# A conditioned decoder layer on one core: cache pages issued three per early gate tile, one operand cut ahead of an evacuation, one activation column behind the exponentials

## The chip, the cores and the metric

One core of a Trainium2 chip runs the whole program. The metric is the device time of that core in microseconds, the median of several runs. TensorE is written PE, VectorE DVE, ScalarE ACT, GpSimd POOL and SyncE SP; ACTq and SPq are the queues on which ACT and SP issue DMAs.

## What is computed

One step of a decoder layer for 256 prompt tokens and 8 sequences of 4 sample tokens, 288 token columns in all, with D_MODEL = 1024 and everything in float32. Cut to what matters here:

```python
h = rms_norm(x, g_norm1) * (1 + scale1) + shift1
q, k, v, qi, ki, wi, u_conv, gates = split(h @ w_in)        # u_conv = [a | g]
z = a * sigmoid(g)                                          # branch B: GLU, then a causal conv of width 31
attn = sparse_attention(q, k, v, qi, ki, wi, cache pages)   # branch A; the samples read 2 cached pages per sequence
x = x + gate1 * ((sigmoid(gA) * (attn @ w_o) + sigmoid(gB) * conv_out) @ w_out)
h2 = rms_norm(x, g_norm2) * (1 + scale2) + shift2
# PEER: 16 picks per head out of 128 x 128 experts
s1, s2 = scores of h2 @ w_q_peer against sub_keys1, sub_keys2
top_s, top_j = top_k(all sums of the best 16 of s1 and of s2, 16)
gate = softmax(top_s)                                       # needs Exp
act = gelu(u_emb[eid] @ h2)                                 # needs Gelu
x = x + gate2 * sum(gate * act * v_emb[eid])
```

The kernel computes the activations of all 16384 experts densely, 128 tiles of 128 experts, and picks afterwards.

## The kernel before

Everything is written by hand, one instruction stream per engine, ordered by semaphores. A weight tile is 128 x 1024 floats (512 KB). SP streams the tiles into a ring of four (`ring`), and the load of a tile waits until the tile four places earlier is done (`tile_done`).

**The head.** `HEAD` is the order of the first products: for k = 0 to 5 the pairs conv_a k, conv_g k, then ki and the four qi tiles, conv_a and conv_g 6 and 7, then v, k and q. After every second tile one tile ("ada", g, s) of the conditioning weights is put in; four of them (s = 0 to 3) make a group g. PE, `linear`, writes tiles other than conv_a alternately into two PSUM banks (`BANK`), and `free` makes PE wait until the tile two places earlier in that order has been evacuated. ACT follows the same list `HEAD`:

- behind a conv_g tile it applies the sigmoid (line 810) and then issues the DMAs of two cache pages, 2m and 2m + 1 for tile m (`load_page`, lines 795 to 797: a register load and four DMAs per page, 32 + 32 + 128 + 128 KB; 16 pages in all);
- behind the last tile of a conditioning group it copies the group (`group_copy`, line 759). PE may not begin the next group before that: `later_ada` waits with `pe.wait_ge(ada_copied, g)`. Group 4 ends behind conv_g 3, and the first tile of group 5 stands behind conv_g 4;
- PE turns the group through a bank (`turn_group`), and ACT copies it out (`turned_copy`, line 765). The turn of group 4 stands behind conv_g 5, ahead of ki; its bank is wanted next by qi 0.

ACT's instructions and the DMAs it issues form one stream in program order. DVE multiplies a and sigmoid(g) (line 1142) and runs the prompt convolution in four pairs of channels (lines 1151, 1155).

**From the PEER queries to the scores.** The 16 tiles peer_q are multiplied in three passes (`linear_cut`: high part by high, high by low, low by high). ACT cuts the high part of a tile into `split` (`cut_tile`, line 781), POOL subtracts it for the low part (line 648), and ACT evacuates each product (`evac`, line 771). Behind the last one PE scores the queries against the sub-keys (line 2072), ACT copies these scores (lines 975, 980), and only then cuts the high part of the first u tile (`cut_high(0, ...)`, line 991). PE needs that high part for `scores(0)` (lines 2095, 2096), and POOL's low part (`cut_low`, line 683) for the last pass (line 2102). PE also waits, ahead of `scores(0)`, for both copies `pscore_copied` and `s_pscore_copied`. `split` has two slots; slot 0 is that of peer_q 14 and of u tile 0, slot 1 that of peer_q 15 and of u tile 1.

**The u tiles.** In each turn of four ACT cuts the next tile's high part and applies gelu to the finished one (line 1020). Behind 16 tiles it applies Exp to the three groups of picks (line 1033), and a loop of three turns follows. The picks' tables are worked out by DVE meanwhile, and PE needs them behind 28 tiles.

Of the kernel before, what the change touches and what calls it, by code (L numbers as in the profile page):

```python
# [21 lines left out]
TP, NSEQ, TD = 256, 8, 4  # L22
# [10 lines left out]
PAGE, NPAGES = 128, 2  # L33
# [78 lines left out]
NRING = len(LOADS)  # L112
# [15 lines left out]
def loaded(pos):  # L128

    return 16 * ((pos - NWIDE) // R + 1)  # L130


def slot_of(c):

    return (NRING + c) % R


def loads_before(c):

    return (NRING + c - NWIDE) // R  # L140
# [27 lines left out]
def tokens(t):  # L168

    return (slice(t * P, t * P + P), P) if t < NQ else (slice(TP, T), TS)  # L170


def build(nc, a):
    f32, f32r, bf16 = mybir.dt.float32, mybir.dt.float32r, mybir.dt.bfloat16
    i32, u32 = mybir.dt.int32, mybir.dt.uint32
    ALU, ACT, AX = mybir.AluOpType, mybir.ActivationFunctionType, mybir.AxisListType

    with ExitStack() as ctx:
        def sb(name, *shape, dt=f32):
            return ctx.enter_context(nc.sbuf_tensor(name, [P] + list(shape), dt))  # L180

        def sem(name):
            return ctx.enter_context(nc.semaphore(name))


        ring = sb("ring", R, D)

        split = sb("split", 2, 2, D, dt=f32r)
# [134 lines left out]
        late = Region(big, NBIG)  # L323
# [10 lines left out]
        tv = late.take(NT, PH, PTOP)  # L334
# [3 lines left out]
        gsum = late.take(NT, PH, 2)  # L338
        eq = late.take(PH * PTOP, PTOP)
        s_expert = late.take(2, TS)  # L340
        assert late.at <= NSUB * TP


# [44 lines left out]
        tile_loaded = [sem(f"tile_loaded{s}") for s in range(R)]  # L388
# [6 lines left out]
        tile_done = sem("tile_done")  # L395
        v_done = sem("v_done")
        u_done = sem("u_done")
        bank_done = sem("bank_done")
        o_done = sem("o_done")
        hi_ready = sem("hi_ready")  # L400
        lo_ready = sem("lo_ready")
        hi_used = sem("hi_used")
# [10 lines left out]
        x_stored = sem("x_stored")  # L413
# [93 lines left out]
        top_exp = sem("top_exp")  # L507
# [109 lines left out]
        def _(pool):  # L617
# [54 lines left out]

            low_tiles(("peer_q",))

            pool.wait_ge(tile_done, NRING)


            def cut_low(c, n, used, value=None):
                pool.wait_ge(hi_ready, c + 1)
                if value is not None:  # L680

                    pool.wait_ge(used, value)
                nc.gpsimd.tensor_tensor(split[:, n % 2, 1], ring[:, slot_of(n), :], split[:, n % 2, 0].bitcast(f32),  # L683
                                        ALU.subtract).then_inc(lo_ready, 1)

            for n in range(R):
                cut_low(n, n, u_done, n - 1 if n >= 2 else None)
            with pool.Fori(1, NSUB // R) as g:
                for n in range(R):
                    cut_low(g * R + n, n, u_done, g * R + (n - 1))  # L690
# [33 lines left out]
        def _(eng):  # L724
# [28 lines left out]
            def group_copy(g):  # L753

                eng.wait_ge(tile_done, POS["ada", g, R - 1] + 1)
                if g >= NFIRST + 2:

                    eng.wait_ge(group_turned, g - NFIRST - 1)
                nc.scalar.activation(m_row2[:, g % 2], adab[:, 0:P], ACT.Copy).then_inc(ada_copied, 1)
# [9 lines left out]
            def evac(key, dst, func=ACT.Copy):  # L769
                eng.wait_ge(tile_done, POS[key] + 1)  # L770
                nc.scalar.activation(dst, lin[BANK[key]][:, 0:T], func).then_inc(act_evac, 1)  # L771

            def cut_tile(key):

                n, at = CUT.index(key), POS[key]
                eng.wait_ge(tile_loaded[at % R], loaded(at))
                if n >= 2:

                    eng.wait_ge(lin_hi_used, n - 1)
                    eng.wait_ge(lin_lo, n - 1)  # L780
                nc.scalar.activation(split[:, n % 2, 0], ring[:, at % R, :], ACT.Copy).then_inc(lin_hi, 1)  # L781
# [17 lines left out]
            for key in HEAD:  # L799
                kind, m = key[:2]  # L800
                if kind == "conv_a":
                    continue
                if kind == "ada":
                    if key[2] == R - 1:
                        group_copy(m)
                elif kind == "turn":
                    turned_copy(m)
                elif kind == "conv_g":
                    eng.wait_ge(tile_done, POS[key] + 1)
                    nc.scalar.activation(sig[:, m], lin[BANK[key]][:, 0:T], ACT.Sigmoid).then_inc(sig_ready, 1)  # L810

                    eng.wait_ge(pages_in, 16)
                    for n in (2 * m, 2 * m + 1):
                        load_page(n)
                elif kind == "ki":
                    evac(key, ki)
                elif kind == "qi":
                    evac(key, qi[:, m])
                elif kind == "v":
                    eng.wait_ge(v_done, m + 1)  # L820
                    rows = tokens(m)[1]
                    nc.scalar.activation(vtok[0:rows, m], lin[BANK[key]][0:rows, 0:VW], ACT.Copy)\
                        .then_inc(act_evac, 1)
                else:
                    n = QK.index(key)
                    if n == len(QK) - 1:
                        cut_tile(("gate_a", 0))
                    evac(key, kT[:, m] if kind == "k" else q[:, m])
                    evac(key, sq_qk[n], ACT.Square)
                    if key == ("q", 3):  # L830

                        eng.wait_ge(z_ready, 2 * KC)
                        nc.scalar.activation(staged_s, zs[:, :, :, TD:TD + LEFT], ACT.Copy).then_inc(conv_staged, 1)
                        nc.scalar.activation(staged_p, zp[:, :, TP:TP + LEFT], ACT.Copy).then_inc(conv_staged, 1)
# [56 lines left out]
            for n in range(NQ * H + 2):  # L891
# [13 lines left out]
                if 1 <= n <= NQ * H:  # L905
                    m = n - 1
# [6 lines left out]
                if n >= 2:  # L913
                    m = n - 2
# [38 lines left out]
            for k in range(KC):  # L953
                eng.wait_ge(h2_ready, k + 2)
                nc.scalar.activation(hi_all[:, k, 0:TP], h2[:, k, 0:TP], ACT.Identity, bias=mod[:, 3, k, 0:1])\
                    .then_inc(rhs_hi, 1)

            eng.wait_ge(stored, 16 * 4)
            for n in range(2 * PH):
                if n + 1 < 2 * PH:  # L960
                    cut_tile(("peer_q", n + 1))
                evac(("peer_q", n), qh[:, n])
                if n == 0:
                    for i in range(2):
                        eng.wait_ge(late_done, i + 1)
                        nc.scalar.activation(m_row2[:, i], pa[1 + i][:, 0:P], ACT.Copy).then_inc(late_copied, 1)
                if n == 2:
                    eng.wait_ge(late_turned, 1)
                    nc.scalar.activation(mod[:, 5], pa[3][:, 0:2 * P].rearrange("p (c g) -> p c g", g=CW_ADA)[:, :, 0:NG],
                                         ACT.Copy).then_inc(late_mod, 1)  # L970
                if n % 4 == 3:
                    for t in range(NQ):
                        m = n // 4 * NQ + t
                        eng.wait_ge(pscore, m + 1)
                        nc.scalar.activation(sc[:, t, n - 3:n + 1], pa[m % 4][:, :].rearrange("p (a b) -> p a b", b=NSUB),
                                             ACT.Copy).then_inc(pscore_copied, 1)
                    if n % 8 == 7:
                        pair = n // 8
                        eng.wait_ge(s_pscore, pair + 1)
                        nc.scalar.activation(sc[:, NQ, 2 * pair:2 * pair + 2],  # L980
                                             (adab, stb)[pair][:, 0:2 * NSUB].rearrange("p (a b) -> p a b", b=NSUB), ACT.Copy)\
                            .then_inc(s_pscore_copied, 1)

            def cut_high(c, n, loaded, first=False):

                eng.wait_ge(tile_loaded[slot_of(n)], loaded)
                if not first:

                    eng.wait_ge(hi_used, c - 1)
                    eng.wait_ge(lo_ready, c - 1)  # L990
                nc.scalar.activation(split[:, n % 2, 0], ring[:, slot_of(n), :], ACT.Copy).then_inc(hi_ready, 1)  # L991

            def gelu(c, n, first=False):

                eng.wait_ge(u_done, c + 1)
                if not first:

                    eng.wait_ge(act_stored[n % 2], 32 * (c // 2))
                nc.scalar.activation(act[:, n % 2], ps[n % 2][:, 0:T], ACT.Gelu_apprx_tanh).then_inc(gelued, 1)

            def first_of(n):
                return 16 * (loads_before(n) + 1)


            eng.wait_ge(x_stored, 16)
            eng.wait_ge(tile_done, NRING)
            cut_high(0, 0, first_of(0), True)
            for c in range(R):
                cut_high(c + 1, (c + 1) % R, first_of((c + 1) % R) + 16 * ((c + 1) // R), c == 0)
                gelu(c, c, c < 2)  # L1010
# [20 lines left out]
            for t in range(NT):  # L1031
                eng.wait_ge(top_max, t + 1)
                nc.scalar.activation(tv[:, t, 0:HEADS[t]], tv[:, t, 0:HEADS[t]], ACT.Exp).then_inc(top_exp, 1)
            with eng.Fori(SOFTMAX // R, TURN // R) as g:
                turn(g, False)

# [1256 lines left out]
```

## Time and profile before

| | us |
|---|---|
| median of 3 runs | 1268.54 (1267.66 to 1269.44) |
| profiled execution, its own time | 1270.7 |
| span of the profiled execution, first to last instruction | 1268.9 |
| busy in it: PE | 1226.8 (97%) |
| DVE | 923.4 (73%) |
| ACT | 570.6 (45%) |
| POOL | 550.5 (43%) |

Times in the rows below are microseconds from the span's start. A row of the timeline has the start, the duration, the engine, the line, the operation with output and input, the count of instructions merged, and in brackets how long the engine had been idle ahead of it and what ended that. ACT_TABLE_LOAD is ACT's change of its function table, with the line of the activation that it is for. "issue" in the brackets means that nothing in the profile was waited for: the engine's own stream had not reached the instruction.

### The profile page before, as it was taken

To read this page: it belongs to the slowest core of one execution; us is meant where nothing else is said; L and a number is where in the kernel's file an instruction comes from. 1 tells how busy PE (TensorE), PEld (TensorE's weight loads), DVE (VectorE), ACT (ScalarE), POOL (GpSimd) and SP (SyncE) were. 2 spreads that over 40 slices of the span, in tenths; PEclk is the share of its full clock that TensorE was granted. 3 is DMA by queue.
4 is the path that set the end of the run, shared out by engine and by line. 5 is a ranking of instruction groups with operands and counts; after the bars stand their busy time and mean duration, and the time that the engine had idled before them with its cause. 6 is when DMAs were issued, how large, how long until landed. Compare 5 with 4: busy or idle time off the path is not lost.

```text
span 1268.9 us, 27584 instructions
## 1 busy us (share of the span) xinstructions
PE 1226.8 (97%) x8591; PEld 1109.1 (87%) x8591; DVE 923.4 (73%) x2246; ACT 570.6 (45%) x991; POOL 550.5 (43%) x272
## 2 busy tenths in 40 slices
PE   5999999999989999999999999999999999999998
PEld 3767677889988999999999999999888888888886
DVE  4499956777743999959999999100467888888866
ACT  2200134656533444654555555444455545545543
POOL 0200015440754567676666666777402444444200
PEclk9999999899998999999999999999999999999999
DMA  9876455332852456665555555667777898888763
GB/s 354 305 240 215 153 192 178 125 121 95 283 180 84 134 163 211 191 207 185 176 186 176 188 184 176 206 208 234 250 239 272 292 348 308 304 299 310 273 230 131
DMA packets 113993, 273.09 MB, mean 215 GB/s; under 512 B 30928, under 2 KB 54192, under 8 KB 113552
## 3 DMA queue, kind: packets, MB, share of 16 engines
q1 hardware_dynamic: 98752, 243.71, 57.0%
q0 software_dynamic: 6432, 19.71, 4.2%
q10 hardware_dynamic: 8752, 8.93, 2.1%
q8 instruction: 32, 0.52, 0.2%
q14 instruction: 25, 0.20, 0.1%
HBM read 249.30 MB, written 23.00 MB: 215 GB/s over the span
## 4 chain that ended last, share of the span: by engine, by line
PE 93%; DVE 2%; DMA 1%; issue 1%; SPq 1%; ACT 1%; POOL 1%; ACTq 0%; DVEq 0%; POOLq 0%
PE ps L2152 19%; PE ps L2102 11%; PE ps L2095 11%; PE ps L2096 10%; PE ps L1724 10%; PE ps L2155 10%; PE ps L1766 5%; PE ps L1776 5%; PE ps L1782 4%; PE ps L2131 2%; DMA ring<-in_stream 1%; PE ps L1798 1%; PE ps L1870 1%; PE ps L2072 1%; SPq L535 1%
## 5 line engine op out<-in xcount | busy, mean ns | idle before, releaser
L683 POOL TENSOR_TENSOR split<-ring,split 128x1024 fp32r<-128x1024 f32 x128 | 307.4, 2403 | 142.1 <-ACT split L991 142.1
L991 ACT ACTIVATE split<-ring 128x1024 fp32r<-128x1024 f32 x256 | 271.5, 1061 | 175.6 <-PE ps L2152 171.2
L2095 PE MATMUL ps<-h2r,split 128*128 128x288 f32 x1024 | 278.7, 297 | 3.1 <-ACT split L991 3.1
L2096 PE MATMUL ps<-h2r,split 128*128 128x288 f32 x1024 | 278.9, 296 | 0.0
L2152 PE MATMUL ps<-h2r,split 128*128 128x512 f32 x1024 | 257.5, 392 | 2.2 <-DVE h2r L1613 2.2
L2152 PEld LDWEIGHTS ps<-h2r,split 128*128 128x128 f32 x1024 | 184.2, 189 | 35.6 <-issue 1.6
L2095 PEld LDWEIGHTS ps<-h2r,split 128*128 128x128 f32 x1024 | 192.9, 188 | 3.6 <-ACT split L991 1.9
L2096 PEld LDWEIGHTS ps<-h2r,split 128*128 128x128 f32 x1024 | 192.5, 188 | 0.0
L648 POOL TENSOR_TENSOR split<-ring,split 128x1024 fp32r<-128x1024 f32 x48 | 118.3, 2467 | 152.6 <-ACT split L781 152.6
L2102 PE MATMUL ps<-h2r,split 128*128 128x288 f32 x1024 | 156.9, 295 | 0.2
L1619 DVE TENSOR_TENSOR split<-ring,split 128x1024 fp32r<-128x1024 f32 x128 | 156.1, 1220 | 0.0
L2155 PEld LDWEIGHTS ps<-h2r,split 128*128 128x128 f32 x1024 | 140.1, 190 | 9.9
L1020 ACT ACTIVATE act<-ps 128x288 f32<-128x288 f32 x124 | 51.0, 412 | 214.0 <-PE ps L2102 211.0
L2155 PE MATMUL ps<-h2r,split 128*128 128x256 f32 x1024 | 143.8, 282 | 0.0
L696 POOL DMA_INDIRECT big<-in_stream,pick_at x32 | 69.6, 2175 | 168.8 <-DVE big L1633 120.4
L2102 PEld LDWEIGHTS ps<-h2r,split 128*128 128x128 f32 x1024 | 141.3, 188 | 1.3 <-POOL split L683 1.2
L1724 PE MATMUL ps<-big,ring 128*128 128x288 f32 x496 | 127.1, 413 | 1.9 <-ACT mod L765 1.9
L1572 DVE SCALAR_TENSOR_TENSOR hot<-ps,parts 128x256 fp32r<-128x256 f32 x256 | 124.3, 485 | 0.0
L1724 PEld LDWEIGHTS ps<-big,ring 128*128 128x128 f32 x496 | 93.4, 192 | 31.6 <-ACT big L771 2.9
L1571 DVE TENSOR_SCALAR hot<-ps,parts 128x128 fp32r<-128x128 f32 x256 | 90.0, 352 | 11.2 <-PE ps L2131 11.2
L1155 DVE SCALAR_TENSOR_TENSOR big<-big 128x256 f32<-128x256 f32 x240 | 95.3, 483 | 0.0
L1607 DVE TENSOR_TENSOR parts<-parts,big 128x256 f32<-128x256 f32 x64 | 27.3, 427 | 82.0 <-DMA parts<-act_dram 81.9
(284 smaller groups left out, 1604.3 us busy)
## 6 DMA issues: line engine op xcount, KB each, us to landing
ring<-in_stream SPq DMA_DIRECT2D x371, 512.0 KB
act_dram<-act SPq DMA_DIRECT2D x128, 128.0 KB, 1.8
big<-in_stream SPq DMA_DIRECT2D x20, 512.0 KB, 7.8
parts<-act_dram SPq DMA_DIRECT2D x16, 512.0 KB
big<-act_dram SPq DMA_DIRECT2D x16, 512.0 KB, 5.3
big<-in_cache_k ACTq DMA_DIRECT2D x16, 128.0 KB, 3.4
big<-in_cache_v ACTq DMA_DIRECT2D x16, 128.0 KB, 3.3
s_act_dram<-act SPq DMA_DIRECT2D x128, 16.0 KB, 1.6
```

The costliest lines, as they stand in the source:

```text
L648: nc.gpsimd.tensor_tensor(split[:, n % 2, 1], ring[:, POS[key] % R, :], split[:, n % 2, 0].bitcast(f32), ALU.subtract).then_inc(lin_lo, 1)
L683: nc.gpsimd.tensor_tensor(split[:, n % 2, 1], ring[:, slot_of(n), :], split[:, n % 2, 0].bitcast(f32), ALU.subtract).then_inc(lo_ready, 1)
L991: nc.scalar.activation(split[:, n % 2, 0], ring[:, slot_of(n), :], ACT.Copy).then_inc(hi_ready, 1)
L1155: ins = V.scalar_tensor_tensor(yp, zp[:, k, j:j + TP], w, yp, ALU.mult, ALU.add)
L1572: return V.scalar_tensor_tensor(hot1[:, slot], iota_ps.unsqueeze(1).to_broadcast([P, 2, P]), parts[:, 0, col], parts[:, 2:4, col].to_broad ...
L1619: V.tensor_tensor(split[:, n % 2, 1], ring[:, slot_of(n), :], split[:, n % 2, 0].bitcast(f32), ALU.subtract).then_inc(lo_ready, 1)
L1724: last = MM(bank[:, 0:T], w[:, k], rhs[:, k], start=(k == 0), stop=(k == KC - 1))
L2095: MM(out, u_hi[:, k], h_hi[:, k], start=(k == 0), stop=False)
L2096: last = MM(out, u_hi[:, k], h_lo[:, k], start=False, stop=False)
L2102: last = MM(out, u_lo[:, k], h_hi[:, k], start=False, stop=(k == KC - 1))
L2152: return MM(ps[k][:, 0:2 * TP], v[0][:, k], w_both, start=first, stop=last)
L2155: return MM(ps[k][:, 0:TP], v[1][:, k], wr[:, n % 2, 0], start=False, stop=False)
```

## The change

- Behind conv_g tile m ACT issues pages 3m to 3m + 2 as long as there are any: three behind each of tiles 0 to 4, one behind tile 5, none behind 6 and 7.
- `cut_high(0, ...)`, with the wait for x's store, moves from behind the score copies to ahead of the evacuation of peer_q 15. It then waits for `NRING - 1` tiles done (peer_q 14) and not for all. POOL's `cut_low` of tile 0 does likewise, and its cut of tile 1 takes the wait for all tiles.
- Behind the three exponentials ACT waits for the first of them and applies gelu to one column of it into a new scratch column, `warm2`.

```diff
@@ POOL
-            pool.wait_ge(tile_done, NRING)
+            pool.wait_ge(tile_done, NRING - 1)
...
-                cut_low(n, n, u_done, n - 1 if n >= 2 else None)
+                cut_low(n, n, *((u_done, n - 1) if n >= 2 else (tile_done, NRING)) if n else (tile_done, NRING - 1))
@@ ACT, head
                     eng.wait_ge(pages_in, 16)
-                    for n in (2 * m, 2 * m + 1):
+                    for n in range(3 * m, min(3 * m + 3, NSEQ * NPAGES)):
                         load_page(n)
@@ ACT, peer_q
             for n in range(2 * PH):
                 if n + 1 < 2 * PH:
                     cut_tile(("peer_q", n + 1))
+                else:
+                    eng.wait_ge(x_stored, 16)
+                    eng.wait_ge(tile_done, NRING - 1)
+                    cut_high(0, 0, first_of(0), True)
                 evac(("peer_q", n), qh[:, n])
...
-            eng.wait_ge(x_stored, 16)
             eng.wait_ge(tile_done, NRING)
-            cut_high(0, 0, first_of(0), True)
             for c in range(R):
@@ ACT, u tiles
                 nc.scalar.activation(tv[:, t, 0:HEADS[t]], tv[:, t, 0:HEADS[t]], ACT.Exp).then_inc(top_exp, 1)
+            eng.wait_ge(top_exp, 1)
+            nc.scalar.activation(warm2, tv[:, 0, 0, 0:1], ACT.Gelu_apprx_tanh)
             with eng.Fori(SOFTMAX // R, TURN // R) as g:
                 turn(g, False)
```

## Rows read from the trace of the kernel before

**Rows 1.** The page, chain of work that ended last, by engine.
```profile
PE 93%; DVE 2%; DMA 1%; issue 1%; SPq 1%; ACT 1%; POOL 1%; ACTq 0%; DVEq 0%; POOLq 0%
```

**Rows 2.** Timeline of ACT and its DMA queue, 40 to 92 us.
```profile
44.66 1.88 ACTq L797 DMA_DIRECT2D big<-in_cache_i  x2
...
63.42 0.39 ACTq L797 DMA_DIRECT2D big<-in_cache_v  x1
...
69.15 1.20 ACTq L797 DMA_DIRECT2D big<-in_cache_i  x2
...
71.79 0.39 ACTq L797 DMA_DIRECT2D big<-in_cache_v  x1
72.22 0.28 ACT L759 ACTIVATE m_row<-ps 128x128 f32<-128x128 f32 x1 [6.30 <-issue]
...
74.72 1.13 ACTq L797 DMA_DIRECT2D big<-in_cache_i  x2
...
77.68 1.15 ACTq L797 DMA_DIRECT2D big<-in_cache_i  x2
...
88.97 0.20 ACT L765 ACTIVATE mod<-ps 128x36 f32<-128x36 f32 x1 [5.99 <-issue]
```

**Rows 3.** Timeline of PE, 25 to 95 us.
```profile
40.38 8.03 PE L1724 MATMUL ps<-big,ring 128*128 128x288 f32 x32
...
73.93 0.65 PE L1798 MATMUL ps<-ring,big 128*32 128x128 f32 x16
...
89.23 4.15 PE L1724 MATMUL ps<-big,ring 128*128 128x288 f32 x16 [1.93 <-ACT mod L765]
```

**Rows 4.** DMA issues: size of each and median us from issue to landing.
```profile
big<-in_cache_k ACTq DMA_DIRECT2D x16, 128.0 KB, 3.4
```

**Rows 5.** The same timeline of PE, at the first dense products.
```profile
30.63 9.24 PE L1724 MATMUL ps<-big,ring 128*128 128x288 f32 x32
```

**Rows 6.** Windows of 2 us, PE: busy, granted clock, DMA share, GB/s.
```profile
30.00:32.00 2.00, 1.82 (x5) 0.50 0.91 322
...
382.00:384.00 2.00, 2.00 (x19) 0.50 0.00 0
...
390.00:392.00 2.00, 2.00 (x11) 0.58 0.00 0
```

**Rows 7.** Timeline of DVE, the first instruction behind the convolution.
```profile
190.03 1.94 DVE L1177 RECIPROCAL big<-big 10x288 f32<-10x288 f32 x1 [14.81 <-ACT big L839]
```

**Rows 8.** Timeline of ACT, 450 to 455 us.
```profile
450.88 0.41 ACT L771 ACTIVATE big<-ps 128x288 f32<-128x288 f32 x1 [2.79 <-PE ps L1782]
...
454.02 0.38 ACT L980 ACTIVATE big<-ps 128x256 f32<-128x256 f32 x1
```

**Rows 9.** Timeline of PE, 455 to 458 us.
```profile
455.49 0.37 PE L2095 MATMUL ps<-h2r,split 128*128 128x288 f32 x1 [1.53 <-ACT split L991]
...
457.95 1.32 PE L2102 MATMUL ps<-h2r,split 128*128 128x288 f32 x8
```

**Rows 10.** Timeline of ACT, behind the exponentials.
```profile
509.68 1.28 ACT L991 ACT_TABLE_LOAD   x1
510.97 1.06 ACT L991 ACTIVATE split<-ring 128x1024 fp32r<-128x1024 f32 x1
```

**Rows 11.** Timeline of PE, the last pass of u tiles around the exponentials.
```profile
509.24 1.23 PE L2102 MATMUL ps<-h2r,split 128*128 128x288 f32 x8
514.57 1.34 PE L2102 MATMUL ps<-h2r,split 128*128 128x288 f32 x8
...
521.09 1.23 PE L2102 MATMUL ps<-h2r,split 128*128 128x288 f32 x8
524.29 1.23 PE L2102 MATMUL ps<-h2r,split 128*128 128x288 f32 x8
527.69 1.32 PE L2102 MATMUL ps<-h2r,split 128*128 128x288 f32 x8
```

**Rows 12.** Waits of DVE, 545 to 860 us: total us, times, longest.
```profile
DVE gate L1563 <- ACT parts L1039: 3.0, 1, 3.0
```

More of the change, by code:

```diff
@@ L340, in build @@
         s_expert = late.take(2, TS)
+        warm2 = late.take(1)
         assert late.at <= NSUB * TP
@@ L956, in _, with cut_high, first_of @@
                     .then_inc(rhs_hi, 1)
+            def cut_high(c, n, loaded, first=False):
+                eng.wait_ge(tile_loaded[slot_of(n)], loaded)
+                if not first:
+                    eng.wait_ge(hi_used, c - 1)
+                    eng.wait_ge(lo_ready, c - 1)
+                nc.scalar.activation(split[:, n % 2, 0], ring[:, slot_of(n), :], ACT.Copy).then_inc(hi_ready, 1)
+            def first_of(n):
+                return 16 * (loads_before(n) + 1)
             eng.wait_ge(stored, 16 * 4)
@@ L982, in _ @@
                             .then_inc(s_pscore_copied, 1)
[L984 to L991, printed above, removed]
             def gelu(c, n, first=False):
@@ L999, in gelu @@
                 nc.scalar.activation(act[:, n % 2], ps[n % 2][:, 0:T], ACT.Gelu_apprx_tanh).then_inc(gelued, 1)
-            def first_of(n):
-                return 16 * (loads_before(n) + 1)
-            eng.wait_ge(x_stored, 16)
             eng.wait_ge(tile_done, NRING)
-            cut_high(0, 0, first_of(0), True)
             for c in range(R):
```

## The prediction

> **What bounds the kernel.** I read the chain that ended last first: PE holds 93% of it [rows 1]. The table of busy times says the same, so time is won or lost only where PE stands still, and each part of the change is priced by what PE waits for at its place. Then I read, for each place, the timelines of PE and of ACT side by side. Three waits of PE are touched: 1.93 us at 89.23 - 1.93 = 87.3 for the turned copy [rows 3], 1.53 us at 453.96 for the first high part [rows 9], and a long step of the u tiles behind the exponentials [rows 11]. One wait that isn't there before decides, I think: the group copy of line 759, which ACT reaches in its own order behind the pages of conv_g 3.
>
> **Part 1, pages: what is removed.** ACT reaches the turned copy at 88.97 only because pages 10 and 11 stand ahead of it; its idle time there reads "issue" [rows 2]. With three pages per tile only page 15 stands there, so this wait of 1.93 us should go.
>
> **Part 1: what is added.** The same stream has another copy in it. Group 4's copy stands behind the pages of conv_g 3. Before, these are eight pages; the last is issued at 71.79 + 0.39 = 72.18 and the copy runs at 72.22, again after "issue" [rows 2]. PE begins group 5, which needs it, at 73.93 [rows 3]: a margin of 73.93 - 72.50 = 1.4 us. After the change twelve pages stand ahead of it. What a page costs ACT's stream:
> - over the first six pages, 44.66 to 63.42 + 0.39 = 63.81, in which the sigmoids hardly wait, 19.15 us; with the missing last gap of about 0.7, 3.3 us a page [rows 2];
> - the shortest step between two pages, 77.68 - 74.72 = 2.96 us [rows 2].
>
> The seventh page is issued after 63.81 at once, since conv_g 2 was finished long before. Six more pages at 2.96 end at 81.6, at 3.3 at 83.6. I take three of each, as the early ones share the DMA engines with the ring's loads and the last ones, with PE standing still, don't: 63.81 + 9.9 + 8.9 = 82.6. The copy (0.28) and its signal let PE go at 83.0. PE stops at 73.93, so the **new stall is 9.1 us**, between 8.0 and 10.1.
>
> **The clock.** A stall of that length costs more than itself. PE's granted clock is 0.50 of full speed, 1.2 GHz, at 30.0 to 32.0, after short stops, and the first 32 dense products take 9.24 us there [rows 5, 6] where the next 32 take 8.03 [rows 3]: 1.2 us. Behind the stall a conditioning tile comes first, whose 16 products also run slow, for some 0.4 us. The wait of 1.93 us at 87.3 itself shows no such loss. I take 1.7 us; the bounds are 0 (no fall) and 5 us (around 382 to 391 the clock stays at 0.50 for some 10 us; the rows show two of its windows [rows 6], and half of it is lost if the products are dense).
>
> **What follows on PE.** From the first tile of group 5 to the end of ki PE needs 87.3 - 73.93 = 13.4 us [rows 3], with the clock's 1.7 more: 83.0 + 13.4 + 1.7 = 98.1. Ki takes the last 4.0 of them (half of the 8.03 of two tiles [rows 3]), so it starts at 94.1. It needs the bank that conv_g 5's sigmoid frees, and ACT must have issued pages 12 to 14 first: 82.6 + 3 x 3.1 = 91.9, in time, though without a loss of clock (ki from 92.4) it would be close. Page 15 and the turned copy come some 3 us behind that sigmoid, while ki runs, so qi 0 starts at 98.1 and not at 89.23: **+8.9 us**. Shortly: 9.1 + 1.7 - 1.93. Does it come back later? The pages that leave tiles 6 and 7 held nobody: PE has no wait there. DVE gets its second sigmoid 3.3 us later and its last pair of channels some 6 us later, but it stands idle for 14.81 us behind the convolution [rows 7], and PE's side of that meeting is later by more. From there on PE, ACT and the ring's loads (which wait for tiles done) follow each other, so I let the whole of it reach the end.
>
> **Part 2, the first high part.** ACT stands idle for 2.79 us, from 448.1 until peer_q 15 is done at 450.9 [rows 8], so the cut (1.06 us, as in rows 10) is hidden there, and POOL's low part (2.4 us) is ready by 451.6. The ring slot of u tile 0 is refilled once peer_q 12 is done, three tiles of 3.2 us ahead of 450.9, at 441.3: over 6 us ahead of the cut. What is late next is the copy of the samples' scores, which ends at 454.02 + 0.38 = 454.40 [rows 8] and for which PE waits too. PE starts at 454.5 and not at 455.49: 1.0 us. Its last pass started 2.46 us behind the first product [rows 9]; a tile's 16 products of the first two passes take 3.20 - 1.07 = 2.13, so up to 0.3 more goes. **-1.2 us**, between -0.9 and -1.4. The second tile's high part starts at 454.3 and its low part is ready at 457.9, before PE wants it at 459.8. If u tile 0 landed late, the cut would hold the last evacuation, and the gain would turn; the 6 us are the cover. DVE, which is busy throughout, falls behind PE by these 1.2 us; its picks are ready early, and it idles 3.0 us behind them for ACT's copies [rows 12], so that cover holds.
>
> **Part 3, the gelu column.** Before, ACT loads a table for the copy at 509.68 (1.28 us) and cuts at 510.97 [rows 10], then loads one more for gelu; both loads come again in each of the two later turns of that loop. PE's step there is 514.57 - 509.24 = 5.33 us, against 524.29 - 521.09 = 3.20 undisturbed, and 527.69 - 524.29 = 3.40 in the next turn [rows 11]; the third turn is like it. After: the load at 509.68 is gelu's, then one column, about 0.2 us (a 128x36 activation is 0.20 [rows 2]), and the cut comes 0.1 to 0.2 later. The long step stays, 0.15 longer; the two steps of 3.40 lose 0.2 each, since loop entry and loop end then agree on the table. **-0.2 us**, between +0.2 and -0.4.
>
> **The sum.** 8.9 - 1.2 - 0.2 = +7.5 us. The profiled execution took 1270.7 us with a span of 1268.9; it would be 1278.2 with 1276.4. It lies 2.2 above the median of the runs, so on the median 1268.54 + 7.5 = **1276.0 us**.
>
> **Rivals.**
> - *The pages don't hold the group copy*, and the change brings what the removed waits say: -1.9 - 1.2 - 0.2 = -3.3, 1265.2 us. It decides in favour if twelve pages are issued in 73.9 - 44.7 = 29.2 us, 2.4 us a page, or less. Against it stands the shortest step of 2.96 us and that both copies read "issue" [rows 2]. The Trainium skill (DMA: Bandwidth & Descriptors, Issuing engines are not separate DMA queues) says that the sequencer's time to start a DMA "is usually small relative to the DMA itself". By that rule ACT would not be held, and this case would come. This trace disagrees: a page's four DMAs take about 3 us of the stream, and one of them lands 3.4 us after its issue [rows 4]. Chance 5%.
> - *The delay is given back*: a later meeting with DVE or with the ring's loads has slack that swallows most of it, for example ACT's waits for ring tiles among the gate_a tiles. Then +8.9 shrinks to 1 or 2 and the sum to about 0: 1268.5 us. Against it: each of those loads waits for a tile that PE finishes. Chance 5%.
> - *Page issue backs up or the clock stays low*: pages 7 to 12 at the step of the slowest one before, 72.18 - 69.15 + 0.7 = 3.7 us [rows 2], put PE's release at 86.4, 3.4 us later; or the clock costs 5 us and not 1.7, 3.3 more. Either gives about 1279.4. For it: the issue times do scatter. Chance 15%.
> - *The release is early and the clock doesn't fall*: pages at 2.96, ki held by ACT alone at 91.4; +6.3 - 1.4 = +4.9, 1273.4. It belongs to the forecast's own range.
>
> **Chances and range.** Forecast with its own spread 75%, slow pages or clock 15%, given back 5%, gain 5%. The range is 1272.5 to 1280.5: from the early release with a little measuring scatter to the third rival with some more; the two 5% cases lie outside. A change within 0.2% (2.5 us) can hardly be told from none: slower by more 90%, the same 5%, faster 5%.
>
> **What the profile after would show.** ACT's group copy behind conv_g 3 near 82.6 after a run of "issue"; PE at the first tile of group 5 idle for about 9 us, released by ACT's copy of line 759; granted clock 0.5 in the windows right behind; no wait of PE for line 765 near the turn of group 4, and qi 0 at about 98; no DMAs of pages behind conv_g 6 and 7. The cut of u tile 0 ahead of the evacuation, and PE's wait ahead of scores(0) 1.0 us shorter, ended by line 980. No table loads inside the loop behind the exponentials. The prediction is wrong if PE shows no wait at group 5, if a page step falls below 2.5 us, or if PE's distance to the old timeline shrinks between 100 and 440 us.

## The result and the profile after

| | before | after |
|---|---|---|
| median of 11 runs each, us | 1269.44 (1267.66 to 1274.01) | 1276.86 (1273.72 to 1280.79) |
| ratio of the times, 95% interval | | 1.0057 (1.0043 to 1.0072) |
| span of the profiled execution, us | 1268.9 | 1275.7 |

The change makes the kernel 0.6% slower, +7.4 us by the medians. The forecast was 1276.0 us: +7.5 on a median of 3 runs, 1268.54, which 11 runs put at 1269.44. Its mechanism is in the trace, and the sizes of several terms are off in ways that nearly cancel.

The chain that ended last, by engine, answers [rows 1]. PE has lost 3 points of it, and ACTq, the issue of DMAs on ACT's queue, has come in:

```profile
PE 90%; DVE 2%; ACTq 2%; DMA 2%; issue 2%; ACT 1%; SPq 1%; POOL 1%; DVEq 0%; POOLq 0%
```

PE's timeline of the head, 60 to 110 us, answers [rows 3]. Line numbers are those of the changed kernel, where the dense products are L1728 and the conditioning tiles L1802:

```profile
83.35 1.08 PE L1802 MATMUL ps<-ring,big 128*32 128x128 f32 x16 [11.42 <-ACT m_row L760]
84.36 9.94 PE L1728 MATMUL ps<-big,ring 128*128 128x288 f32 x32
94.14 0.27 PE L1829 MATMUL ps<-ident,m_row 128*128 128x128 f32 x1
94.34 0.64 PE L1802 MATMUL ps<-ring,big 128*32 128x128 f32 x16
94.91 8.03 PE L1728 MATMUL ps<-big,ring 128*128 128x288 f32 x32
102.87 0.65 PE L1802 MATMUL ps<-ring,big 128*32 128x128 f32 x16
```

The first row is the new wait: 11.42 us ahead of the first tile of group 5, released by the group copy. The second row is conv_a 5 and conv_g 5, 9.94 us where the same number of products takes 8.03 in the row at 94.91. That row holds ki and qi 0 without a gap: the 1.93 us for the turned copy [rows 3] are gone. These two tiles now take 102.87 - 94.91 = 7.96 us. Before, they took 93.31 - 83.15 = 10.16, so the wait was worth 2.2 us and not only its 1.93:

```profile
83.15 4.15 PE L1724 MATMUL ps<-big,ring 128*128 128x288 f32 x16
...
93.31 0.64 PE L1798 MATMUL ps<-ring,big 128*32 128x128 f32 x16
```

ACT and its DMA queue, 40 to 105 us, answer [rows 2]:

```profile
46.17 1.24 ACTq L798 DMA_DIRECT2D big<-in_cache_i  x2
...
70.66 2.12 ACTq L798 DMA_DIRECT2D big<-in_cache_i  x2
...
82.59 0.39 ACTq L798 DMA_DIRECT2D big<-in_cache_v  x1
83.02 0.28 ACT L760 ACTIVATE m_row<-ps 128x128 f32<-128x128 f32 x1 [8.67 <-issue]
...
94.34 0.41 ACT L811 ACTIVATE big<-ps 128x288 f32<-128x288 f32 x1 [10.74 <-PE ps L1728]
...
97.32 0.20 ACT L766 ACTIVATE mod<-ps 128x36 f32<-128x36 f32 x1 [2.57 <-issue]
```

Twelve pages end at 82.98, 36.8 us after the first began, 3.1 us each. From 55 us on each page's issues follow the last one's within 0.8 us; in the program there stand between them only the register load of the page's number and, behind every third page, a sigmoid. One page took longer, the ninth: 4.0 us, of which the first two issues alone took 2.12 us. The group copy follows the twelfth page at once. PE had asked for it 11 us before.

PE in windows of 2 us (busy, granted clock, DMA share, GB/s) shows the clock, as [rows 6] do for before:

```profile
72.00:74.00 2.00, 0.00 (x0) 1.00 0.72 226
74.00:76.00 2.00, 0.00 (x0) 0.65 0.80 261
76.00:78.00 2.00, 0.00 (x0) 0.50 0.52 145
...
86.00:88.00 2.00, 2.00 (x6) 0.50 0.94 338
88.00:90.00 2.00, 2.00 (x9) 0.94 0.58 157
```

It falls to 0.50, 1.2 GHz, while PE stands still, and comes back at about 88 us, some 5 us after PE began again.

Around the first u tile (PE, 460 to 466 us) the row that answers [rows 9] is:

```profile
463.86 0.37 PE L2099 MATMUL ps<-h2r,split 128*128 128x288 f32 x1 [0.54 <-ACT big L992]
```

The wait is 0.54 us and not 1.53. The bracket names line 992, but PE waits there for both score copies; the copy of line 997 runs from 463.38 to 463.76, and that end fits PE's start at 463.86.

The last passes around the exponentials (PE, 500 to 530 us), against [rows 11]:

```profile
517.28 1.23 PE L2106 MATMUL ps<-h2r,split 128*128 128x288 f32 x8
522.69 1.33 PE L2106 MATMUL ps<-h2r,split 128*128 128x288 f32 x8
525.99 1.23 PE L2106 MATMUL ps<-h2r,split 128*128 128x288 f32 x8
...
529.19 1.09 PE L2106 MATMUL ps<-h2r,split 128*128 128x288 f32 x7
```

The long step is 5.41 us (before 5.33), then come 3.30 and 3.20; no step of 3.40 is left, and ACT has no table load inside that loop.

**Where the time went.** The distance between the two timelines, after minus before, at points that both have:

| point | after minus before, us |
|---|---|
| PE ready for group 5 (71.94 against 73.93) | -2.0 |
| PE begins group 5 (83.35 against 73.93) | +9.4 |
| PE behind qi 0 (102.87 against 93.31) | +9.6 |
| ACT's group copy (212.91 against 203.34) | +9.6 |
| a cut of ACT (361.53 against 353.55) | +8.0 |
| peer_q 15 evacuated (460.24 against 450.88) | +9.4 |
| first gelu (467.35 against 459.31) | +8.0 |
| last gelu ahead of the exponentials (515.35 against 507.31) | +8.0 |
| gelus some ten tiles later (549.65 against 542.12) | +7.5 |
| end of the span | +6.8 |

The first row is no effect of the change: in this execution PE began its dense products 0.8 us earlier and ran the first of them at the full clock, 7.94 us and not 9.24. Such scatter in the head, and again between 220 and 395 us, moves single traces of these kernels by up to 4 us. Where the granted clock stood explains a part of it; for the rest I have no cause. So sizes below a few us are read from timelines and not from whole times.

### The profile page after: what moved, and what is told of

Read it like the earlier page. It is cut to its first block, busy times and chain, and to the rows that moved or that the text cites. A ratio compares the mean times of both kernels' runs of the same rounds, so it can differ in the third digit from the quotient of the medians.

```text
span 1275.7 us, 27584 instructions
## 1 busy us (share of the span) xinstructions
PE 1225.1 (96%) x8591; PEld 1108.1 (87%) x8591; DVE 920.3 (72%) x2246; ACT 564.3 (44%) x987; POOL 546.6 (43%) x272
## 4 chain that ended last, share of the span: by engine, by line
PE 90%; DVE 2%; ACTq 2%; DMA 2%; issue 2%; ACT 1%; SPq 1%; POOL 1%; DVEq 0%; POOLq 0%
PE ps L2156 18%; PE ps L2106 10%; PE ps L2099 10%; PE ps L2100 10%; PE ps L2159 10%; PE ps L1728 9%; PE ps L1770 5%; PE ps L1780 4%; PE ps L1786 4%; PE ps L2135 2%; ACTq L798 2%; DMA ring<-in_stream 1%; PE ps L1802 1%; PE ps L1874 1%; POOL split L684 1%
## 5 line engine op out<-in xcount | busy, mean ns | idle before, releaser
L697 POOL DMA_INDIRECT big<-in_stream,pick_at x32 | 63.9, 1998 | 172.9 <-DVE big L1637 125.5
L1728 PE MATMUL ps<-big,ring 128*128 128x288 f32 x496 | 127.5, 414 | 0.0
L1728 PEld LDWEIGHTS ps<-big,ring 128*128 128x128 f32 x496 | 93.7, 192 | 29.9 <-ACT big L772 2.9
```

The costliest lines, as they stand in the source:

```text
L1728: last = MM(bank[:, 0:T], w[:, k], rhs[:, k], start=(k == 0), stop=(k == KC - 1))
```

## The experiments

Ratios are against runs of the kernel before on the same chip in the same session, with 95% intervals.

**Pages alone.**

```diff
-                    for n in (2 * m, 2 * m + 1):
+                    for n in range(3 * m, min(3 * m + 3, NSEQ * NPAGES)):
```

> The kernel before with the pages three per tile, nothing else. Theory (ACT's stream, with the group copy behind twelve pages, holds PE; clock falls): all of the loss and none of the gains, about +9 us on the kernel before, 1278 us; PE idle 9 to 11 us ahead of the first tile of group 5, released by the copy of line 759; wait of 1.5 us ahead of scores(0) still there. Rival (the loss comes from the moved high part or the gelu column): about the time before or 2 us less.

1277.18 us against 1270.05, ratio 1.0048 (1.0030 to 1.0066). PE in its head:

```profile
82.59 1.08 PE L1798 MATMUL ps<-ring,big 128*32 128x128 f32 x16 [8.63 <-ACT m_row L759]
83.60 10.36 PE L1724 MATMUL ps<-big,ring 128*128 128x288 f32 x32
```

The stall stands there with this part alone, 8.63 us from 73.96; PE arrived later than in the changed kernel, and the release came at nearly the same time, 82.6 against 83.3. The release is set by ACT's stream. The gap of the whole time, +7.1, is 2 less than the expected 9, and its interval (3.8 to 8.4 us) ends below it. By whole times this kernel can't be told from the changed one (1.0048 and 1.0057), which has the two gains besides; what the stall costs is read from the timelines: behind qi 0 PE is 9.2 us later here than before (102.53 against 93.31).

**The group copy ahead of conv_g 3's pages.** This asks whether the copy's place is the cause or only where the cause shows.

```diff
-                    if key[2] == R - 1:
+                    if key[2] == R - 1 and m > NFIRST:
                         group_copy(m)
...
                     eng.wait_ge(pages_in, 16)
+                    if m == R - 1:
+                        group_copy(NFIRST)
                     for n in range(3 * m, min(3 * m + 3, NSEQ * NPAGES)):
                         load_page(n)
```

> The changed kernel with group 4's copy ahead of conv_g 3's pages instead of behind them: nine pages stand ahead of the copy, fifteen still ahead of conv_g 5's sigmoid. Theory A (the sum of page issues on ACT's stream is the limit, and the group copy is only the first place where it shows): the stall of 11.4 us shrinks to 1 to 3, and a new one of 7 to 8 us appears ahead of ki, released by ACT's sigmoid of conv_g 5 near 92.4; the time stays within 1.5 us of the changed kernel, 1275 to 1277 us. Theory B (the group copy alone is the cause): the stall goes and nothing takes its place; the three gains stay, about 1266 us.

1277.65 us, ratio 1.0059 (1.0039 to 1.0079): as slow as the changed kernel. PE and then ACT:

```profile
73.93 0.65 PE L1804 MATMUL ps<-ring,big 128*32 128x128 f32 x16 [2.01 <-ACT m_row L760]
74.51 9.72 PE L1730 MATMUL ps<-big,ring 128*128 128x288 f32 x32
...
91.97 9.61 PE L1730 MATMUL ps<-big,ring 128*128 128x288 f32 x32 [7.06 <-ACT big L811]
```

```profile
91.07 0.39 ACTq L798 DMA_DIRECT2D big<-in_cache_v  x1
91.50 0.41 ACT L811 ACTIVATE big<-ps 128x288 f32<-128x288 f32 x1 [8.55 <-issue]
```

Theory A, to within a microsecond (91.5 where 92.4 was expected): 2.0 us at group 5, then 7.06 ahead of ki, behind the sigmoid of conv_g 5 at 91.5, which in turn stands behind page 14. The clock now falls twice (9.72 and 9.61 for 32 products). So the limit is the sum of page issues on ACT's stream; whichever of ACT's copies PE asks for first only names it.

**Two pages moved behind the turned copy.** Two per tile as before, pages 10 and 11 behind the turned copy; the other two parts as changed.

```diff
                     turned_copy(m)
+                    if m == NFIRST:
+                        for n in (10, 11):
+                            load_page(n)
...
-                    for n in range(3 * m, min(3 * m + 3, NSEQ * NPAGES)):
+                    for n in (2 * m, 2 * m + 1) if m != 5 else ():
                         load_page(n)
```

> Two pages per tile as before, but the two of conv_g 5 behind group 4's turned copy instead of ahead of it; the first high part and the gelu column as changed. Theory: no stall at group 5, no wait for the turned copy (1.93 us less), clock stays up there, ki's evacuation behind the two pages at about 89.5 and in time; with the gains of the two other parts 3 to 4 us faster than before, about 1266 us. Rival (PE's progress in the head is set by something else, so an earlier turned copy is given back): 1.5 to 2 us faster only, 1268 us.

1265.83 us against 1270.05, ratio 0.9970 (0.9954 to 0.9986), 4.2 us faster than before, 3 to 4 expected. PE runs from group 5's start through ki and qi 0 without a gap; the tile ahead of ki, and ki with qi 0:

```profile
80.71 0.65 PE L1805 MATMUL ps<-ring,big 128*32 128x128 f32 x16
81.28 8.03 PE L1731 MATMUL ps<-big,ring 128*128 128x288 f32 x32
```

**The move alone**, on the kernel before:

> The kernel before with only the two pages of conv_g 5 moved behind group 4's turned copy. Theory: the wait of 1.9 us for line 765 goes and nothing takes its place; 1.9 us faster than before, 1268.3 us. Rival: given back, 1270.2 us.

1266.02 us against 1268.96, ratio 0.9979 (0.9965 to 0.9992). Its trace has no wait of PE for the turned copy in the head:

```profile
82.71 8.03 PE L1727 MATMUL ps<-big,ring 128*128 128x288 f32 x32
90.66 0.65 PE L1801 MATMUL ps<-ring,big 128*32 128x128 f32 x16
```

Ki and qi 0 take 7.95 us where they took 10.16: 2.2 us gained. By the medians it is 2.9 us, 1.0 to 4.4 by the interval: the expected 1.9 lies inside, and the rival (nothing) doesn't. The profiled execution was this kernel's slowest, 1270.64 us, with a span of 1268.8 like that of before; what it had gained by 103 us was lost again between 220 and 395 us, where the traces scatter.

**Pages issued by POOL.** `load_page` moved to POOL's stream, behind its low part of h; ACT issues none.

```diff
+            pool.wait_ge(pages_in, 16)
+            for n in range(NSEQ * NPAGES):
+                load_page(n)
+
             pool.wait_ge(conv_staged, 2)
```

> The changed kernel with all pages issued by POOL behind its low part of h, none by ACT. Theory (it is the issue time on ACT's stream that costs, not the bytes or their time of landing): no stall at group 5 and none at the turned copy; 3 to 4 us faster than before, about 1266 us, as turn_first. Rival (earlier pages cost because their bytes compete with the ring's loads): PE waits for ring tiles between 45 and 130 us, and the time stays above that of before.

> pool_pages once more, to see whether its 1263.2 us from 5 runs holds. If its lead over turn_first is real, 1263 to 1264 us; if it is scatter by where the clock falls, 1265 to 1266 us.

1263.22 us (5 runs), ratio 0.9945 (0.9928 to 0.9962), and 1263.64 us (12 runs), ratio 0.9957 (0.9944 to 0.9970). This beats both kernels. POOL's first and last page, and ACT's copies without them:

```profile
39.59 1.08 POOL L641 DMA_DIRECT2D big<-in_cache_i  x2
...
79.66 0.54 POOL L641 DMA_DIRECT2D big<-in_cache_v  x1
```

```profile
65.78 0.28 ACT L770 ACTIVATE m_row<-ps 128x128 f32<-128x128 f32 x1 [0.19 <-PE ps L1802]
...
82.55 0.20 ACT L776 ACTIVATE mod<-ps 128x36 f32<-128x36 f32 x1
```

Here the pages are issued earlier and faster than by the change, the first at 39.6 and not 46.2 us, sixteen in 40.6 us, 2.5 us each, and PE waits for no ring tile. The window from 45 to 75 us for this kernel and then for the changed one (busy, clock, DMA share, GB/s):

```profile
45.00:75.00 30.00, 30.00 (x176) 1.00 0.98 322
```

```profile
45.00:75.00 30.00, 26.93 (x150) 0.99 0.83 277
```

The DMA engines are nearly full, 0.98, and PE is never idle. So the bytes' earlier arrival costs nothing; the issue time on the stream that also holds PE's copies does.

**The same on the kernel before:**

> The kernel before with only the pages moved to POOL. If all that matters is that ACT's stream is free, as turn_only: 1268.3 us. If POOL as issuer brings something more (as the gap between pool_pages and turn_first hints: 2.6 us), 1265 to 1266 us, and the trace must show a second wait of PE that is shorter.

1265.18 us against 1268.96, ratio 0.9978 (0.9961 to 0.9995), as the move alone (0.9979). Its time lies in the range of the rival, 1265 to 1266 us, but the move alone, 1266.02, came out at its edge too, and no second wait that is shorter was found: behind qi 0 both traces are ahead of the kernel before by about the same, 2.5 and 2.6 us. So POOL as issuer brings nothing more than ACT's free stream, as far as this can be measured. The repeat, 1263.64 us, came out where a real lead was expected to. But the kernel before was 1.1 us faster in that session too, and by the ratios (0.9957, and 0.9970 for turn_first) the intervals overlap. The traces show no lead either: the first gelu starts at 455.15 us in turn_first, at 455.00 in the repeat and at 453.58 in the first run of the same kernel. So the lead isn't shown to be real.

**PE kept busy through the stall.** In the changed kernel, ahead of PE's wait for group 4's copy:

```diff
                 if s == 0 and g > NFIRST:
+                    if g == NFIRST + 1:
+                        pe.wait_ge(stat_r, 1)
+                        for i in range(36):
+                            MM(stb[:, 0:T], ones[:, :], hT[:, i % KC], start=True, stop=True)
                     pe.wait_ge(ada_copied, g)
```

> The changed kernel with 36 products of 128 x 128 by 288 columns, whose result nobody reads, ahead of PE's wait for group 4's copy; they take some 9 us of a stall of 11. Theory (the stall also costs by the clock): the granted clock stays at 1.00 through 76 to 92, conv_a 5 and conv_g 5 take 8.03 us and not 9.94, the conditioning tile 0.65 and not 1.08, and the run is 2.3 us faster than the changed kernel, 1274.5 us, though the products do no useful work. Rival (the slow products behind the stall come from late ring tiles or from ACT): those durations stay, and the time does too.

1281.84 us, ratio 1.0091 (1.0070 to 1.0112): 5 us slower than the changed kernel, against the expectation. My count was wrong, not the mechanism:

```profile
74.10 17.62 PE L1824 MATMUL ps<-big,ones 128*128 128x288 f32 x72
91.65 0.65 PE L1802 MATMUL ps<-ring,big 128*32 128x128 f32 x16
92.23 8.03 PE L1728 MATMUL ps<-big,ring 128*128 128x288 f32 x32
```

36 products are 72 instructions, one every 0.245 us, and PE begins the conditioning tile at 91.65, 8.3 us later than in the changed kernel. The two rows behind them already show the theory's durations. With half of the products (`range(18)`):

> As keep_busy, but with 18 products: each of them runs as two passes of 0.245 us, so 36 had taken 17.6 us and outlasted the stall; 18 should take 8.8 and end before ACT's copy at about 83. Theory (the clock is a part of the loss of its own): granted clock 1.00 through 76 to 92, conv_a 5 and conv_g 5 in 8.03 us, the conditioning tile in 0.65, PE's release unchanged; 2.3 us faster than the changed kernel, 1274.5 us. Rival (keeping PE busy there changes nothing in sum): 1276.9 us.

1274.37 us, ratio 1.0050 (1.0032 to 1.0067). PE, then two of its windows:

```profile
72.05 8.89 PE L1824 MATMUL ps<-big,ones 128*128 128x288 f32 x36
83.15 0.65 PE L1802 MATMUL ps<-ring,big 128*32 128x128 f32 x16 [2.21 <-ACT m_row L760]
83.72 8.03 PE L1728 MATMUL ps<-big,ring 128*128 128x288 f32 x32
```

```profile
76.00:78.00 2.00, 2.00 (x10) 1.00 0.63 190
...
86.00:88.00 2.00, 2.00 (x10) 1.00 0.90 324
```

PE is released at the same time as after the change (83.15 against 83.35), so the stall of useful work is unchanged, yet the tile takes 0.65 and not 1.08 and the pair 8.03 and not 9.94: 0.43 + 1.91 = 2.3 us are the clock's share. Behind qi 0 this trace is 7.0 us behind the kernel before (100.32 against 93.31), where the changed kernel is 9.6. The whole times don't settle it: 1274.4 against 1276.9 fits, but they are of different sessions, and the ratios, 1.0050 and 1.0057, differ by only 0.9 us with overlapping intervals. So the clock's share rests on these rows. The products do no useful work; this prices the clock, and it is no version to keep.

**Without the pages, and each other part alone.**

> The change without its part on the pages: first high part moved and gelu column added. By the trace of the changed kernel they bring 1.3 and 0.5 us: 1.8 us faster than before, about 1267.7 us. If the moved cut or its waits cost elsewhere, within 0.5 us of before.

1267.52 us against 1270.26, ratio 0.9983 (0.9970 to 0.9997): 2.7 us faster, 1.8 expected and inside the interval (0.4 to 3.8).

> Only the first high part and POOL's waits moved. PE's wait ahead of scores(0) falls from 1.5 to 0.5 us, ended by the copy of the samples' scores, and the first gelu comes 1.3 us earlier against the end of the peer_q tiles. The table loads behind the exponentials stay as before, seven of them with the steps of 5.3 and twice 3.4 us.

> Only the gelu column. The long step behind the exponentials becomes 0.1 to 0.2 us longer, the two steps of 3.4 us fall to 3.2 and the wait of 1.5 us ahead of scores(0) stays; ACT has four table loads fewer; 0.2 to 0.5 us faster from the exponentials to the gates, below what the time of the whole kernel can tell.

Whole times can't tell either from none (0.9995, 0.9975 to 1.0015; and 0.9999, 0.9981 to 1.0017), so I read the timelines of ACT. With the cut moved, peer_q 15's evacuation and the first gelu:

```profile
450.11 0.41 ACT L772 ACTIVATE big<-ps 128x288 f32<-128x288 f32 x1 [1.84 <-PE ps L1784]
...
457.21 0.41 ACT L1007 ACTIVATE act<-ps 128x288 f32<-128x288 f32 x1 [1.33 <-PE ps L2104]
```

7.10 us apart; with the gelu column alone, as before, more:

```profile
449.85 0.41 ACT L772 ACTIVATE big<-ps 128x288 f32<-128x288 f32 x1 [2.79 <-PE ps L1785]
...
458.31 0.41 ACT L1000 ACTIVATE act<-ps 128x288 f32<-128x288 f32 x1 [1.75 <-PE ps L2105]
```

8.46 us apart. The moved cut brings 1.3 to 1.4 us, as expected. In warm_only the steps of the last passes around the exponentials are 5.40, 3.33 and then 3.20 throughout; in cut_only they are 5.31, 3.29, 3.20, 3.20, 3.39, 3.29. The two parts act apart. Cut_only has the seven table loads of before in that stretch (one for Exp, three for the copy, three for gelu). Warm_only has two, those for Exp and for the new column: five fewer, and not the four that I had expected.

## Why the prediction was right, step by step

- **The added wait.** Twelve pages ahead of the group copy, end forecast at 82.6, measured 82.98; PE's release forecast at 83.0, measured 83.35. Confirmed by pages_only (82.6). In part this match is luck: ACT began its first page 1.5 us later than before (46.17 against 44.66), which is scatter, and its twelve pages took 36.8 us where the forecast had 37.9. Pages_only, which began at 44.51, took 37.7. Most steps between pages lie between 2.95 and 3.3 us, as assumed, and the ninth page's was 4.0, longer than the 3.7 of the rival with slow pages. The stall itself was 11.42 and not 9.1 (bounds 8.0 to 10.1) in the profiled execution, almost all because PE came 2.0 us earlier; PE's start of group 5 moved by 9.4.
- **The removed wait.** The turned copy no longer holds PE; turn_only shows the gain by itself. It was taken at its idle time, 1.93 us, and was worth 2.2.
- **The clock.** Taken at 1.7 us with bounds of 0 and 5; measured 2.3. The row I leaned on [rows 5] was 9.24 against 8.03, and there the clock came back at about 33 us, 3 us into the products. Behind the stall it stayed low until about 88, so the loss in the dense pair was 1.91 and not 1.2.
- **The close call at ki.** I had sigmoid 5 in time for ki, with ACT's stream close behind. In the changed kernel it was in time (94.34, directly behind PE); page 14 was issued by 91.96, forecast 91.9. Copy_first shows that without the first stall it would have been the next to hold PE.
- **Qi 0.** Forecast 98.1. The pair of ki and qi 0 starts at 94.91 and takes 8.03, so qi 0 starts near 98.9.
- **Nothing comes back.** +9.56 behind qi 0 and +9.57 at 203 us, a hundred us later: DVE's meeting behind the convolution gave nothing back, as said. Between 220 and 395 us the distance moved down to +8.0 and up again, and it was +9.4 at 460. By the letter that is one of the signs of being wrong that the prediction names (a distance that shrinks between 100 and 440 us). Part of it is the clock, which in the kernel before was at 0.50 around 225 to 228 us and in the changed one, at the same work, was not; for the fall of 0.9 us between 320 and 355 I have no cause. A return of up to about 1 us is therefore not excluded.
- **The first high part.** -1.2 forecast, -1.3 measured (+9.36 to +8.04). PE's next holder was the copy of the samples' scores.
- **The gelu column.** -0.2 forecast with an edge of -0.4; measured +0.08 - 0.30 - 0.27 = -0.5. The missed term: a step of PE that was held is followed by one that is 0.1 longer too (3.29 to 3.33 and not 3.20), so removing a hold of 0.2 saves 0.3.
- **The sum.** +7.5 forecast, +7.4 by the medians. By the terms as measured, 9.4 + 2.3 - 2.2 - 1.3 - 0.5 = +7.7, and the traces have +7.5 at 550 us. The stall was taken too low by 0.3 and the clock by 0.6, the three gains together by 0.7, so that the sum is nearer than its terms. The last 0.7 us of difference between the traces lies behind 860 us, where PE's waits for DVE's low parts are 1.4 and not 2.2 in sum; I have no run that ties this to the change.
- **The rival of the Trainium skill's rule** (DMA: Bandwidth & Descriptors, Issuing engines are not separate DMA queues: the time to start a DMA is usually small relative to the DMA itself) fell, but the rule itself didn't, and "this trace disagrees" was a wrong reading. For one DMA the trace agrees: a row of issue takes 0.4 to 0.6 us for most of them, and a DMA of 128 KB lands 3.4 us after its issue [rows 4]. What the rival drew from it doesn't follow: twelve pages are 48 such starts and 12 register loads in one stream, 3.1 us a page, and small times add up to 36.8 us ahead of the copy. What that section says besides, that issuing from several engines "will only save the time on the sequencer", is what pool_only and turn_only show together: POOL as issuer brought no more than the free stream did.

## What to carry to other kernels

A DMA is cheap for the engine that issues it only if nothing that others wait for stands behind it: count the issues ahead of each copy in an in-order stream, multiply by their measured step (here 3 us a page), and compare with the time at which the consumer asks. A wait that reads "issue" on a helper engine was cured here by moving issues behind the copy, or to another engine's stream, and not by bunching them elsewhere ahead of other copies. When a stall is added to PE, price the clock that it costs as well, and when a place is blamed, move it once: if the stall turns up at the next place, the limit is the stream.

## What the runs showed of the hardware that I had not expected

- A stall of 11.4 us cost another 2.3 us by the clock, and 18 filler products prevented it. The wait of 1.93 us at 87.3 in the kernel before cost none, nor did one of 2.21 us in the run with 18 products; yet one of 2.01 us in copy_first was followed by a slow pair of products, 9.72 us for 8.03. What separates them I didn't test.
- One float32 product of 128x128 by 288 columns is two instructions on PE, and they follow each other every 0.245 us (72 in 17.62 us in the run with 36 products).
- POOL's stream issued a page in 2.5 us on average, in steps of 2.1 to 3.1, ACT's in about 3.1.
- A table load that is not in the kernel's text stood in front of a plain copy inside the loop behind the exponentials, once per turn, and went when a gelu column stood ahead of the loop (warm_only). That it had stood there because the loop's entry and end held different tables is argued, not shown. The load took 1.28 us with no visible pause on either side [rows 10].
